# The gates move between the experts' two products, and the rows are added back in two fp32r passes

## The reference, cut to what matters

```
def hier_moe(h, ...):          # group top-1, then expert top-2 inside the group
    gates = pg * pv / sum(pv);  expert_id = gi * 8 + pi
    return grouped_experts(xf, expert_id, gates, w_gu, w_down)

def grouped_experts(xf, expert_id, gates, w_gu, w_down):
    # rows of each expert gathered into blocks
    a, b = split(x_rows @ w_gu[e])               # 1024 -> 2 x 512
    y_rows = (silu(a) * b) @ w_down[e]           # 512 -> 1024
    return segment_sum(y_rows[dest] * gate[:, None], token)   # times the gate, added to the token's row
```

## Time and profile before

| | us |
|---|---|
| median of three runs | 2534.71 |
| the profiled execution | 2531.46 |
| its span on the core | 2529.7 |
| PE busy | 2218.7 (88%) |
| PE weight loads | 1793.3 (71%) |
| DVE busy | 1136.5 (45%) |
| ACT busy | 884.1 (35%) |

### The profile page before, as it was taken

One profiled execution on the slowest core, in us unless ns is written; L12 is line 12 of the kernel. 1 busy time (PEld: TensorE's weight loads), 2 busy tenths in 40 slices (PEclk: granted clock), 3 DMA queues, 4 the chain that ended last, 5 costly groups with the idle time before them and its releaser, 6 DMA issues. The chain is left out here.

```text
span 2529.7 us, 45042 instructions
## 1 busy us (share of the span) xinstructions
PE 2218.7 (88%) x19490; PEld 1793.3 (71%) x19490; DVE 1136.5 (45%) x2008; ACT 884.1 (35%) x1470; POOL 58.3 (2%) x78
## 2 busy tenths in 40 slices
PE   6998788887885999869999998787898998898998
PEld 6967466654553996757777776554778997777997
DVE  5355345223422643543333323424746555746554
ACT  4443332233211442322222222333444444544442
POOL 0000000000000000000000000000000000000000
PEclk8999898999998999989999999787988999988999
DMA  6594998999999557559999999797413555413551
GB/s 237 167 321 173 357 380 343 397 402 404 403 400 371 183 184 266 216 211 378 414 414 416 412 413 367 307 358 273 145 34 122 183 173 166 138 46 123 183 174 38
DMA packets 254367, 676.26 MB, mean 267 GB/s; under 512 B 12624, under 2 KB 65872, under 8 KB 254160
## 3 DMA queue, kind: packets, MB, share of 16 engines
q1 hardware_dynamic: 238832, 614.77, 64.4%
q0 software_dynamic: 15328, 58.50, 6.0%
HBM read 672.17 MB, written 1.05 MB: 266 GB/s over the span
## 5 line engine op out<-in xcount | busy, mean ns | idle before, releaser
L444 PE MATMUL bank<-xx,high 128*128 128x256 f32 (+1 forms) x3296 | 636.3, 294 | 38.3 <-DVE xx L583 25.8
L444 PEld LDWEIGHTS bank<-xx,high 128*128 128x128 f32 (+1 forms) x3296 | 526.4, 195 | 95.4 <-issue 69.5
L444 PE MATMUL bank<-xx,low 128*128 128x256 f32 (+1 forms) x1648 | 476.2, 289 | 0.0
L444 PEld LDWEIGHTS bank<-xx,low 128*128 128x128 f32 (+1 forms) x1648 | 322.2, 196 | 1.6
L393 DVE TENSOR_TENSOR low<-lane,high 128x1024 fp32r<-128x1024 f32 (+1 forms) x112 | 130.7, 1170 | 346.6 <-ACT high L382 346.6
L382 ACT ACTIVATE high<-lane 128x1024 fp32r<-128x1024 f32 (+1 forms) x112 | 113.0, 1012 | 322.8 <-PE bank L444 322.8
L444 PE MATMUL bank<-hx,high 128*128 128x256 f32 x1056 | 199.6, 290 | 0.0
L444 PEld LDWEIGHTS bank<-hx,high 128*128 128x128 f32 x1056 | 165.8, 192 | 17.7 <-issue 15.1
L444 PE MATMUL bank<-hx,low 128*128 128x256 f32 x528 | 149.8, 284 | 0.0
L1335 ACT ACTIVATE hs<-bank 64x256 f32<-64x256 f32 x64 | 24.2, 378 | 297.8 <-PE bank L1322 297.8
L1342 DVE TENSOR_TENSOR hs<-hs,bank 64x256 f32<-64x256 f32 x64 | 27.1, 423 | 212.7 <-ACT hs L1335 212.7
(11 more groups left out here) (547 smaller groups left out, 4086.9 us busy)
## 6 DMA issues: line engine op xcount, KB each, us to landing
ring__13<-in_expert_w_gu SPq DMA_DIRECT2D x52, 1024.0 KB, 10.4
ring__12<-in_expert_w_gu SPq DMA_DIRECT2D x51, 1024.0 KB, 10.9
ring__14<-in_expert_w_gu SPq DMA_DIRECT2D x51, 1024.0 KB, 10.5
ring__56<-in_expert_w_gu SPq DMA_DIRECT2D x26, 1024.0 KB, 11.2
ring__12<-in_expert_w_down SPq DMA_DIRECT2D x26, 1024.0 KB, 8.6
ring__154<-in_expert_w_gu SPq DMA_DIRECT2D x26, 1024.0 KB, 11.1
ring__55<-in_expert_w_gu SPq DMA_DIRECT2D x25, 1024.0 KB, 10.8
ring__14<-in_expert_w_down SPq DMA_DIRECT2D x25, 1024.0 KB, 9.7
```

Source lines behind the costliest of these rows:

```text
L444: done = pe.matmul(out, a.bitcast(F32R), b.bitcast(F32R), start=it["start"] and k == 0 and q == 0 and not halves, stop=stop)
```

## The change

Four things are changed. (1) The gates are no longer in the scatter's one-hots. Two matmuls with a matrix of ones (`gates`, in `scatter_pe`) spread each row's gate over all partitions, ACT copies that to `gs`, and DVE multiplies it in when it moves the turned hidden rows from PSUM to `ht` (`across_dve`, in place of `across_act`). (2) The scatter's one-hots are now exact in fp32r; three more copies are written by DVE (`d_r`), and they are turned by fp32r matmuls with an identity. (3) The result of the second product is split: ACT writes its high part in fp32r, DVE then subtracts to get the low part, and PE adds back both parts, 16 fp32r matmuls in place of 8 fp32 ones. (4) `ht` and `y` have one buffer each in place of two, and some buffers share space differently.

```diff
         row, ones_r, pick = space(ctx, "row", NROW), space(ctx, "ones_r", 1), space(ctx, "pick", 16)
-        mods = space(ctx, "mods", 256)
+        mods, ident_r = space(ctx, "mods", 256), space(ctx, "ident_r", P)
...
                 act.activation(pick.bitcast(F32R), V("pick"), ACT.Copy)
+                act.activation(ident_r.bitcast(F32R), ident, ACT.Copy)
...
         up_p, up_a, up_v = sig("up_mm"), sig("up_silu"), sig("up_gated")
-        ac_p, ac_a, dn_p, dn_v, bk_p = sig("hidden_turned"), sig("hidden_copied"), sig("down_mm"), sig("down_copied"), sig("back_mm")
+        ac_p, ac_v, dn_p, dn_v, bk_p = sig("hidden_turned"), sig("hidden_copied"), sig("down_mm"), sig("down_copied"), sig("back_mm")
         moe_x = sig("moe_added")
+        gn_p, gn_a, yh_a = sig("gate_spread_mm"), sig("gate_spread"), sig("down_high")
...
         def moe(L, before, opened, early_name, x_ready, beside, places, cut):
...
             lane = Lane(room)
-            xt, tmp, rs, xn, wr = room("xt", KC, T), room("tmp", KC, T), room("rs", T), room("xn", 2, DM), room("wr", KC, 36)
+            xt, rs, xn = room("xt", KC, T), room("rs", T), room("xn", 2, DM)
+            stack, get = room.part()
+            wr = get("wr", KC, 36)
+            stack.close()
+            d_r, dg_t = room("d_r", 2, GB, 4 * SL).rearrange("p a b (h s) -> p a b h s", h=4), room("dg_t", 2, GB, SL)
+            d_t = d_r[:, :, :, 0, :]
+            stack, get = room.part()
+            tmp = get("tmp", KC, T)
+            stack.close()
+            dts = room("dts", 2, GB, T)
...
             ohj, ohk = (xt.rearrange("p a t -> p (a t)")[:, o:o + NX * NE].rearrange("p (j n) -> p j n", j=NX) for o in (DM, DM + NX * NE))
-            dt_b = Turns(halves(tmp, "p (b t) -> p b t", b=GB), kept)
-            d_t, dg_t = room("d_t", 2, GB, SL), room("dg_t", 2, GB, 4, SL)
+            dt_b = Turns([dts[:, i] for i in range(2)], kept)
+            gs_b = Turns([room("gs", GB, SL) for _ in range(2)], kept)
             hs_b = Turns([room("hs", 256) for _ in range(2)], kept)
-            ht_b = Turns([room("ht", 2, 2, SL) for _ in range(2)], kept)
-            y_b = Turns([room("y", 256) for _ in range(2)], kept)
+            ht_b = Turns([room("ht", 2, 2, SL)], kept)
+            y_b = Turns([room("y", 2, 256)], kept)
...
                     dve.wait_ge(*gath_p.at(K(q - 1, 4)))
+                    dve.wait_ge(*dt_p.at(K(q - 1, (min(GB, NB - GB * (q - 1)) - 1) // 2)))
                 for a in range(2):
-                    i = dve.tensor_tensor(d_t[:, a, 0:n, :], bc(iota[:, 0:SL], [P, n, SL], 1),
+                    i = dve.tensor_tensor(d_t[:, a, 0:n, :].bitcast(F32R), bc(iota[:, 0:SL], [P, n, SL], 1),
...
                 i.then_inc(*oh_v.up(K(q, "d")))
+                for a in range(2):
+                    i = dve.tensor_tensor(d_r[:, a, 0:n, 1:4, :].bitcast(F32R), bc(iota[:, 0:SL], [P, n, 3, SL], 1, 1),
+                                          bc(px[:, a, GB * q:GB * q + n], [P, n, 3, SL], 2, 3), ALU.is_equal)
+                i.then_inc(*oh_v.up(K(q, "rows")))
...
                 if q:
-                    dve.wait_ge(*dt_p.at(K(q - 1, (min(GB, NB - GB * (q - 1)) - 1) // 2)))
+                    dve.wait_ge(*gn_p.at(K(q - 1)))
                 for a in range(2):
-                    i = dve.tensor_tensor(dg_t[:, a, 0:n], bc(d_t[:, a, 0:n], [P, n, 4, SL], 2),
-                                          bc(gx[:, a, GB * q:GB * q + n], [P, n, 4, SL], 2, 3), MUL)
+                    i = dve.tensor_tensor(dg_t[:, a, 0:n], d_t[:, a, 0:n], bc(gx[:, a, GB * q:GB * q + n], [P, n, SL], 2), MUL)
...
             def scatter_pe(pe, q):
...
                         pe.wait_ge(*s.at(k))
-                    pe.wait_ge(*oh_v.at(K(q, "g")))
+                    pe.wait_ge(*oh_v.at(K(q, "rows")))
...
                         for a in range(2):
-                            i = pe.transpose(bank[:, j * T + a * P:j * T + (a + 1) * P], dg_t[:, a, b + j].rearrange("p d s -> p (d s)"), ident)
+                            i = pe.matmul(bank[:, j * T + a * P:j * T + (a + 1) * P], d_r[:, a, b + j].rearrange("p h s -> p (h s)").bitcast(F32R),
+                                          ident_r.bitcast(F32R), start=True, stop=True)
                     i.then_inc(*dt_p.up(K(q, b // 2)))
+                key = K("gates", q)
+                bank = pq.next(key)
+                for s, k in pq.freed(key):
+                    pe.wait_ge(*s.at(k))
+                pe.wait_ge(*oh_v.at(K(q, "g")))
+                for a in range(2):
+                    i = pe.matmul(bank[:, 0:n * SL], ones, dg_t[:, a, 0:n], start=a == 0, stop=a == 1)
+                i.then_inc(*gn_p.up(K(q)))
...
             def scatter_out(e, q, which, ev):
...
                         e.wait_ge(*bk_p.at(K(GB * (q - 1) - 1)))
-                    o, s = d[:, b:b + m, :], pq[key][:, 0:m * T].rearrange("p (a t) -> p a t", a=m)
+                    o, s = d[:, b:b + m, :].bitcast(F32R), pq[key][:, 0:m * T].rearrange("p (a t) -> p a t", a=m)
...
                     pq.free(key, (ev, K(q, b)))
+                if which:
+                    key, g = K("gates", q), gs_b.next(K(q))
+                    e.wait_ge(*gn_p.at(K(q)))
+                    for s, k in gs_b.freed(K(q)):
+                        e.wait_ge(*s.at(k))
+                    e.activation(g[:, 0:n, :], pq[key][:, 0:n * SL].rearrange("p (b s) -> p b s", s=SL), ACT.Copy).then_inc(*gn_a.up(K(q)))
+                    pq.free(key, (gn_a, K(q)))
...
             def gathered(q):
...
-            def across_act(act, b):
-                ht, key = ht_b.next(K(b)), K("across", b)
-                act.wait_ge(*ac_p.at(K(b)))
+            def across_dve(dve, b):
+
+                ht, key, g = ht_b.next(K(b)), K("across", b), gs_b[K(b // GB)][:, b % GB, :]
+                dve.wait_ge(*ac_p.at(K(b)))
+                dve.wait_ge(*gn_a.at(K(b // GB)))
                 for s, k in ht_b.freed(K(b)):
-                    act.wait_ge(*s.at(k))
-                act.activation(ht, pq[key][:, 0:128].rearrange("p (k h s) -> p k h s", k=2, h=2), ACT.Copy).then_inc(*ac_a.up(K(b)))
-                pq.free(key, (ac_a, K(b)))
+                    dve.wait_ge(*s.at(k))
+                dve.tensor_tensor(ht.rearrange("p k h s -> p (k h) s"), pq[key][:, 0:128].rearrange("p (a s) -> p a s", s=SL),
+                                  bc(g, [P, 4, SL], 1), MUL).then_inc(*ac_v.up(K(b)))
+                pq.free(key, (ac_v, K(b)))
+                if b % GB == GB - 1 or b == NB - 1:
+                    gs_b.free(K(b // GB), (ac_v, K(b)))
...
             def down_pe(pe, b, part):
...
                         pe.wait_ge(*s.at(k))
-                    pe.wait_ge(*ac_a.at(K(b)))
+                    pe.wait_ge(*ac_v.at(K(b)))
...
+            def down_act(act, b, part):
+                if part < 1:
+                    return
+                y, key = y_b.next(K(b)), K("down", b)
+                act.wait_ge(*dn_p.at(K(b, 1)))
+                for s, k in y_b.freed(K(b)):
+                    act.wait_ge(*s.at(k))
+                act.activation(y[:, 0, :].bitcast(F32R), pq[key][:, 0:256], ACT.Copy).then_inc(*yh_a.up(K(b)))
+
             def down_dve(dve, b, part):
...
                     return
-                y, key = y_b.next(K(b)), K("down", b)
-                dve.wait_ge(*dn_p.at(K(b, 1)))
-                for s, k in y_b.freed(K(b)):
-                    dve.wait_ge(*s.at(k))
-                dve.tensor_copy(y, pq[key][:, 0:256]).then_inc(*dn_v.up(K(b)))
+                y, key = y_b[K(b)], K("down", b)
+                dve.wait_ge(*yh_a.at(K(b)))
+                dve.tensor_tensor(y[:, 1, :].bitcast(F32R), pq[key][:, 0:256], y[:, 0, :], SUB).then_inc(*dn_v.up(K(b)))
...
             def back_pe(pe, b):
...
                     pe.wait_ge(*acc_v.at(K(3)))
-                for j in range(2):
+                for j, part in ((0, 0), (1, 0), (0, 1), (1, 1)):
                     for h in range(4):
-                        i = pe.matmul(acc_b[h][:, j * T:(j + 1) * T], y[32 * h:32 * h + 32, j * P:(j + 1) * P],
-                                      d[32 * h:32 * h + 32, b % GB, :], start=False, stop=True, tile_position=(32 * h, 0),
+                        i = pe.matmul(acc_b[h][:, j * T:(j + 1) * T], y[32 * h:32 * h + 32, part, j * P:(j + 1) * P].bitcast(F32R),
+                                      d[32 * h:32 * h + 32, b % GB, :].bitcast(F32R), start=False, stop=True, tile_position=(32 * h, 0),
...
                 fs = [none, lambda q: prepare_out(act, q, True, gath_a), lambda q: scatter_out(act, q, True, dt_a),
-                      lambda b, k: up_act(act, b, k), lambda b: across_act(act, b), none, none]
+                      lambda b, k: up_act(act, b, k), none, lambda b, k: down_act(act, b, k), none]
...
                 route(dve)
```

(4 more changed lines are left out.)

## The result

| | before | after |
|---|---|---|
| median, us (runs) | 2535.77 (4) | 2557.79 (4) |
| lowest to highest, us | 2528.01 to 2537.45 | 2555.55 to 2565.96 |
| profiled execution: span, us | 2529.7 | 2555.9 |
| mean granted TensorE clock | 0.928 | 0.922 |
| PE busy, us (share) | 2218.7 (88%) | 2217.0 (87%) |

PE is TensorE at matmuls, DVE VectorE, ACT ScalarE, and SP the engine that issues the loads of weights. The granted clock is given as a share of 2.4 GHz; at 0.5, 1.2 GHz, a matmul takes twice as long. "A down" is one of the two quarters, 16 records each, of a block's second product.

What follows compares the result with a forecast made beforehand. Weights set the pace in the second layer (1194 to 1494 us), the ring's slots in first-layer turns 4 to 11. 14.8 of waits - 2.6 - 6.5 + 0.6 = 6.3, taken as 6: 2534.7 + 6 = 2541 us, range 2523 to 2556.

Steps and rivals of the forecast that it cites:

- Waits forecast as 4.4, 3.5, 3.9, 3.0 and 1.8 us: PE's down product waits for DVE's `ht`: first-layer turns 4, 5, 7, 9, then every fourth turn of the second layer.
- The add-back: In 64 blocks, 16 fp32r matmuls take 0.65 us where 1.08 stood: 0.43 us less a block.
- The one-hots: In 16 groups on DVE, six instructions take 2.0 us, 0.25 more than before.
- The scatter's group: In 16 groups on PE, 8 fp32r matmuls plus two for the gates take 1.27 us, 0.3 more than before.
- What of it reaches the end: First layer, turns 4 to 11: 14.8 us of waits - 2.6 add-backs - 6.5 slack + 0.6 scatter = 6.3; second layer nothing.
- slack: First layer, turns 4 to 11: PE's waits for weights, 5.1 + 1.4 = 6.5 us, can take up new waits.
- that stretch: First layer, turns 4 to 11, 327 to 482 us, DMA share 0.91: the ring holds the weights back; 6.3 us lost.
- The first rival: First-layer turns 4, 5, 7, 9: lower clock behind each new wait costs 4 x 3 = 12 us more, 2553; chance 0.25.
- Elsewhere small gains and waits, taken as nothing: Outside first-layer turns 4 to 11 and the second layer's 1194 to 1494 us: no net effect, 0 us.
- the second rival: Where DMA share is below 1.02, PE's work sets the pace: 30 blocks give back 0.43 us each, 13 us, 2522; chance 0.15.
- The second layer: 1194 to 1494 us: 0.4 us a group against 11 us idle, weights keep the pace at DMA share 1.02, nothing lost.
- The third rival: First layer: the ring hides all the waits, PE catches up after each, time stays at 2535; chance 0.15.

Runs made afterwards that it cites:

- fill_waits: The changed kernel with 14 dummy fp32 matmuls on PE in the waits of first-layer turns 4, 5, 7 and 9: 2543.15 us, ratio 1.0041.
- ht_by_act: The changed kernel with `ht` copied by ACT again and the gate left out of the result, gates still spread: 2536.68 us, ratio 1.0016.
- rows_only: The kernel before with only the add-back in two fp32r passes, gates in the one-hots, `ht` by ACT: 2525.09 us, ratio 0.9938.
- ht_by_act_no_gates: The changed kernel with `ht` copied by ACT, the gate left out and the whole gate spread removed: 2522.40 us, ratio 0.9944.
- before_ht_on_dve: The kernel before with one edit, the copy to `ht` done by DVE and not ACT: 2543.50 us, ratio 1.0029.

## Why the prediction was wrong

**The sizes of waits and instructions were right, but for the scatter's.** Waits forecast as 4.4, 3.5, 3.9, 3.0 and 1.8 us came as 4.62, 3.92, 4.58, 3.50 and 2.03. The add-back, start to start, took 0.67 us (in the rows below) where 0.65 was forecast and 1.08 stood before. The 1.7 us that the rule of the Trainium skill would give ("TensorE: Matmul & The Clock Gate", section "LDWEIGHTS (loading the stationary operand)", 107 ns for each of 16 loads) did not come. The one-hots took 0.49 + 1.02 + 0.49 = 2.0 us, as forecast. The scatter's group was low in the forecast, 1.27; PE in turn 10 of the second layer of the changed kernel, against the earlier trace rows:

```profile
1345.08 1.09 PE L1295 MATMUL bank<-ident_r,d_r 128*128 128x128 f32 x8
1346.02 0.71 PE L1304 MATMUL bank<-dg_t,vec 128*128 128x128 f32 x4
1346.66 0.34 PE L1383 MATMUL bank<-vec,hs 64*128 64x64 f32 x2
...
1348.55 0.74 PE L1446 MATMUL bank<-dts,y 32*128 32x256 f32 x16
1349.22 1.07 PE L1412 MATMUL bank<-ring__15,ht 128*32 128x256 f32 x16
```

0.94 + 0.64 = 1.58 us, 0.6 more than before in place of 0.3. The 8 fp32r matmuls save nothing against 8 transposes (0.97): 0.12 us each, for 128 columns as for 256. By the same section of the Trainium skill a weight load of 128 columns takes 107 ns; the 0.12 us of the trace, at full height of 128 rows, is near it, though no run shows that the loads set the pace.

**The step that failed is "What of it reaches the end".** It made 6 us of the waits, less add-backs and slack. The turns of that stretch lost 16.8. The term that it left out of the sum, at nothing, is the clock behind the four waits. fill_waits shows it: with the waits as long but the clock kept, the stretch loses 6.2 us. So the forecast of 6 fits the length, in one trace, and the clock was the rest: 10 to 11 us in the traces, 15 by the ratios, give or take 9. (The slack was taken from two rows; the same view has a third wait for weights, 0.7 us for `ring__55`, by which the sum would be 0.7 lower.) The first rival had this mechanism, its place and its price (12 us); it should have been in the sum, since the earlier trace rows showed it at a wait of 4.07 us and all four new waits were near that size, 3.50 to 4.62. What was said against it, that weights still to land would hide the slower PE, cannot hold in a stretch that had been chosen because the weights wait for PE.

**A second step failed unnoticed.** "Elsewhere small gains and waits, taken as nothing" was a gain of 15 us from the add-back and a loss of 18 from the gate spread, of which the scatter's 0.3 us a group was all that was forecast. The 15 us are near the price of the second rival, 13, but the agreement is in part luck: of its 30 blocks the traces show the gain at the 13 in the second layer only. The two cancel in ht_by_act (+4), so the end looked as if neither were there. What remains of the 25 us is `ht` on DVE, 21. The middle column is the forecast's sum; the right one follows one order of taking the parts away, from rows_only to the changed kernel:

| by the ratios, us | forecast | shown |
|---|---|---|
| add-back, fp32r | -2.6 | -15 (rows_only) |
| fp32r scatter | 0 | +1 (ht_by_act_no_gates; its turning alone +7) |
| gate spread | +0.6 | +18 (of it the matmuls 12) |
| `ht` behind DVE's queue | +8.3 | +21 (of it the clock 10 to 15) |
| sum | +6 | +25 |

The parts don't simply add: `ht` on DVE costs 21 us when it is the last part put in, and 7 in the kernel before alone. That its place starts the waits, and that the clock is the larger part of their price, is shown; why the rest of the change makes that price three times as high is not.

**The second layer** held nearly as forecast: 2.03 us five times, DMA share 1.02, stretch 303 us for 300. **The third rival** (all hidden) is out.

## What to carry over

When a change makes TensorE wait, ask for two prices: the wait, less the slack; and what TensorE does in the microseconds behind it at half clock. The second was the larger here; one pair of rows in the trace of the kernel before had shown it, and a few dummy matmuls in the wait tell the two apart in one experiment. A change of several parts that comes out near nothing may hold a gain: take the parts alone, and count added matmuls on the engine that sets the pace at their full time.

## What the runs showed of the hardware

- Behind the four waits of PE of 3.5 to 4.6 us the clock was at its lower level for about 6 us each time (a down of 1.93 for 1.07 us). With dummies in the wait it stayed up. Over both MoE layers of all fourteen traces, a part of a product (16 records) behind a wait of 3.5 us or more took 1.85 us or more in 14 of 15 cases; behind a wait of 2.0 to 2.5 us it did so in 25 of 82, and took its 1.07 of the full clock in 42.
- Row-tiled fp32r matmuls of 256 columns, 32 rows high, four tiles: 16 in 0.67 us, 0.04 each; fp32r matmuls with full 128-row loads took 0.12 us each, no faster at 128 columns than fp32 transposes.
- PE stopped for 5.0 to 6.0 us at a branch, with no releaser in the profile, and 64 more records of PE in the program made a second stop of 2.8 to 4.5 us appear.
- One kernel's times spread by 10 to 20 us with the mean clock granted (before_ht_on_dve: 0.934 at 2536.8, 0.923 at 2557.3 us; the kernel before beside it: 0.929 at 2523.9, 0.923 at 2544.9). In one profiled execution the same code behind both layers took 6.8 us less than in another.
